# Token scalars transposed into another PSUM bank, the prologue's loads and low parts in another order, some of VectorE's low parts asked for one slab sooner

## What is computed

```python
for l in range(DEPTH):
    h = _rms_norm(x, norm_mix_pre[l])
    y = _hybrid_mixer(h, positions, w_in[l], conv_w[l], a_log[l], dt_bias[l], gdn_norm[l], w_out[l], topk)
    x = x + _rms_norm(y, norm_mix_post[l])
    h = _rms_norm(x, norm_x_pre[l])
    mem_n = _rms_norm(mem, norm_mem[l])
    y = _memory_cross_attention(h, mem_n, w_xq[l], w_xkv[l], w_xo[l])
    x = x + _rms_norm(y, norm_x_post[l])
    h = _rms_norm(x, norm_ffn_pre[l])
    y = _swiglu(h, w_gu[l], w_down[l])
    x = x + _rms_norm(y, norm_ffn_post[l])
```

```python
q = _rope(a_q.reshape(B, S, ATT_HEADS, ATT_HEAD_DIM), positions)
k = _rope(a_k.reshape(B, S, ATT_KV_HEADS, ATT_HEAD_DIM), positions)
qi = _rope(i_q.reshape(B, S, IDX_HEADS, IDX_DIM), positions)
ki = _rope(i_k.reshape(B, S, 1, IDX_DIM), positions)[:, :, 0]
y_a = _dsa_attention(q, k, v, qi, ki, i_w * (IDX_HEADS ** -0.5), topk)
qkv = _causal_conv_silu(b_qkv, conv_w)          # four taps, then silu
o_b = _gated_delta_rule(bq, bk, bv, g, beta)
y = jax.nn.sigmoid(g_a) * y_a + jax.nn.sigmoid(g_b) * y_b
return y @ w_out
```

## Time and profile before

| | |
|---|---|
| runs | 1144.62, 1144.62, 1147.76 us |
| the profiled execution | 1147.81 us, its span 1146.0 us |
| PE busy | 1121.3 us, 98% of the span |
| POOL, ACT, DVE busy | 678.3, 567.2, 559.1 us |
| mean granted clock of TensorE | 0.993 of full speed |
| chain that ended last | PE 92%; DMA 2%; DVE 2%; ACT 1%; POOL 1% |

### The profile page before, as it was taken

How to read it: one execution, slowest core, us unless ns; L and a number is a source line. 1 busy time by engine, 2 the same in 40 slices (tenths; PEclk the granted TensorE clock), 3 DMA queues, 4 the chain that set the end, 5 groups by cost and what they waited for, 6 DMA issues and landing times.

```text
span 1146.0 us, 19832 instructions
## 1 busy us (share of the span) xinstructions
PE 1121.3 (98%) x8108; PEld 1043.6 (91%) x8112; DVE 559.1 (49%) x1042; ACT 567.2 (49%) x894; POOL 678.3 (59%) x355
## 2 busy tenths in 40 slices
PE   8899999999999899999998999999999999999997
PEld 6899999998798799999998999999988978999997
DVE  5678566445412543534545856683634235211333
ACT  7445764434554534444463467543445545444443
POOL 4776567617684347754586658575187634576433
PEclk9899999999999999999998999999999999999999
DMA  7344334524543545555553444455155344555553
GB/s 280 130 165 148 131 133 161 176 65 151 203 149 127 178 170 184 184 185 185 185 177 134 148 143 153 123 176 161 40 199 185 129 149 160 188 184 184 184 183 112
DMA packets 63338, 183.41 MB, mean 160 GB/s; under 512 B 18576, under 2 KB 19088, under 8 KB 63248
## 3 DMA queue, kind: packets, MB, share of 16 engines
q1 hardware_dynamic: 47936, 172.51, 42.9%
q10 hardware_dynamic: 15312, 9.64, 3.1%
HBM read 179.51 MB, written 2.62 MB: 159 GB/s over the span
## 4 chain that ended last, share of the span: by engine, by line
PE 92%; DMA 2%; DVE 2%; ACT 1%; POOL 1%; issue 1%; SPq 0%; DVEq 0%; POOLq 0%; ACTq 0%
PE psum L476 26%; PE psum L477 26%; PE psum L478 26%; DMA sb_raw<-weights 2%; PE psum L613 1%; PE psum L904 1%; PE psum L883 1%; PE psum L657 1%; PE psum L640 1%; PE psum L550 1%; PE psum L789 1%; PE psum L796 1%; PE psum L624 1%; PE psum L750 1%; PE psum L741 1%
## 5 line engine op out<-in xcount | busy, mean ns | idle before, releaser
L379 POOL TENSOR_TENSOR sb_low<-sb_raw,sb_high 128x1024 fp32r<-128x1024 f32 x261 | 627.7, 2416 | 355.3 <-ACT sb_high L369 347.0
L369 ACT ACTIVATE sb_high<-sb_raw 128x1024 fp32r<-128x1024 f32 x322 | 340.4, 1061 | 468.0 <-DMA sb_raw<-weights 406.6
L476 PE MATMUL psum<-sb_h_high,sb_high 128*128 128x256 f32 x1664 | 472.0, 284 | 1.3 <-DVE sb_low L379 1.3
L478 PE MATMUL psum<-sb_h_high,sb_low 128*128 128x256 f32 x1664 | 469.7, 282 | 0.0
L477 PE MATMUL psum<-sb_h_low,sb_high 128*128 128x256 f32 x1664 | 469.3, 282 | 0.0
L476 PEld LDWEIGHTS psum<-sb_h_high,sb_high 128*128 128x128 f32 x1664 | 314.4, 189 | 3.7 <-issue 2.2
L477 PEld LDWEIGHTS psum<-sb_h_low,sb_high 128*128 128x128 f32 x1664 | 313.3, 188 | 0.9
L478 PEld LDWEIGHTS psum<-sb_h_high,sb_low 128*128 128x128 f32 x1664 | 312.6, 188 | 0.0
L379 DVE TENSOR_TENSOR sb_low<-sb_raw,sb_high 128x1024 fp32r<-128x1024 f32 x61 | 94.2, 1557 | 30.0 <-ACT sb_high L369 29.5
L1926 DVE SCALAR_TENSOR_TENSOR sb_sq<-sb_th,psum 128x512 f32<-128x512 f32 x22 | 15.1, 688 | 140.3 <-ACT sb_th L1360 140.3
L1697 DVE SCALAR_TENSOR_TENSOR sb_conv<-psum,sb_param,sb_conv 128x255 f32<-128x255 f32 (+1 forms) x144 | 58.3, 474 | 48.6 <-ACT sb_conv L1172 48.5
(11 more groups left out here) (278 smaller groups left out, 1594.0 us busy)
## 6 DMA issues: line engine op xcount, KB each, us to landing
sb_raw<-weights SPq DMA_DIRECT2D x322, 512.0 KB, 3.2
sb_pre_gain<-pre_gains ACTq DMA_DIRECT2D x6, 512.0 KB, 5.1
sb_post_gain<-post_gains ACTq DMA_DIRECT2D x6, 512.0 KB, 3.7
sb_kx<-mem SPq DMA_DIRECT2D x2, 512.0 KB, 4.3
sb_x<-x SPq DMA_DIRECT2D x1, 1024.0 KB, 11.2
t_dram<-sb_sq ACTq DMA_DIRECT2D x4, 256.0 KB, 2.9
out<-sb_x SPq DMA_DIRECT2D x4, 256.0 KB, 2.1
m_dram<-sb_m ACTq DMA_DIRECT2D x8, 64.0 KB, 2.0
```

The lines of the kernel that those rows point to most:

```text
L369: nc.scalar.activation(high[:, n % HIGHS, :], raw[:, n % RAWS, :], ACT.Copy).then_inc(high_ready, 1)
L379: eng.tensor_tensor(low[:, k, :], raw[:, k, :], high[:, n % HIGHS, :].bitcast(F32), ALU.subtract).then_inc(low_ready[k], 1)
L476: pe.matmul(out, a[0], b[0], start=start, stop=False, **kw)
L478: return pe.matmul(out, a[1], b[0], start=False, stop=stop, **kw)
```

## The change

It has four pieces.

1. The token scalars are transposed into bank 3 in place of bank 6. Bank 3 holds the angles while the rotary tables are made, in layer 0; no claim of the layer has used it by then.
2. SP loads slabs 0, 1, 2, then x, then the positions, then slabs 3 and 4. Low part 3 is now DVE's. ACT makes high part 3 after the squares of x. In DVE's `prenorm` a call `low_parts(4)` is added behind the loop over the two tiles, under the condition that the loop's variable `c` is 0; the loop leaves it at 1, so the call is not made.
3. In the norm behind `out`, DVE asks for low parts up to two slabs ahead of `out` in place of one, ahead of the wait for the sum of squares.
4. Ahead of the first `silu` of the feed-forward part DVE asks for low parts up to three slabs ahead in place of two.

```diff
-            return n in (0, 2, HALVES + 4) or (part, i, b) in (("xv", 2, 0), ("xv", 2, 1), ("xv", 3, 0), ("xo", 3, 1))
+            return n in (0, 2, 3, HALVES + 4) or (part, i, b) in (("xv", 2, 0), ("xv", 2, 1), ("xv", 3, 0), ("xo", 3, 1))
...
             for n in range(RAWS):
+                sp.dma_start(raw[:, n, :], weights[n]).then_inc(raw_loaded[n], 16)
                 if n == 2:
+                    sp.dma_start(x, x_in.rearrange("(c p) d -> p c d", p=P)).then_inc(x_loaded, 16)
                     sp.dma_start(y_t[:, 0:S].bitcast(I32), pos_in.broadcast_to([P, S])).then_inc(pos_loaded, 16)
-                    sp.dma_start(x, x_in.rearrange("(c p) d -> p c d", p=P)).then_inc(x_loaded, 16)
-                sp.dma_start(raw[:, n, :], weights[n]).then_inc(raw_loaded[n], 16)
...
                 wide(("k", 0), h, (dve_rope, "k"))
-                o = claim("small_tok", (dve_gate, "x"), (6,))
+                o = claim("small_tok", (dve_gate, "x"), (3,))
                 pe.wait_ge(*act_copy.at(layer, "small"))
...
-            highs(act, done, HIGHS)
+            highs(act, done, HIGHS - 1)
...
                         square_x("mix", c, half)
                 if layer == 0:
+                    highs(act, done, HIGHS)
                     for j in range(4):
...
+                    if (layer, which, c) == (0, "mix", 0):
+                        low_parts(4)
                     if between is not None:
                         between()
...
-                        low_parts(ahead(product, 2 if part == "x" else 1))
+                        low_parts(ahead(product, 2))
...
                 for i in range(FF_SLOTS):
-                    low_parts(ahead(("gate", i), 2))
+                    low_parts(ahead(("gate", i), 2 if i else 3))
```

## The result

The changed kernel takes 1153.85 us (median of 7 runs, 1150.26 to 1155.72), where the kernel before takes 1145.76 us on the same chip (7 runs, 1143.39 to 1148.2). The ratio is 1.0067, with a 95% interval of 1.0054 to 1.0081: slower by 7.7 us by the ratio, by 8.1 between the medians. The forecast was 1153.7 us.

The account below looks back on a forecast made before the run. PE, busy 1121.3 of 1146.0 us, bounds the kernel, so only its standstills and half clock matter. 1147.8 - 12.2 + 8.2 + 5.1 + 5.8 + 1.9 - 2.95 = 1153.7 us; range of 8 in 10: 1147.8 to 1157.5.

Parts of the forecast that it names:

- waits and half clock at L568: Token-scalar transposes, both layers: PE's two 3.03 us waits and the 3.1 and 3.05 us of clock go, -12.2 us.
- `bv 0` standing still: First matmul of bv 0 waits for DVE's taps of bq 3, 4.13 and 4.06 us by layer, +8.2 us.
- half clock at `bv 0`: PE's clock falls in each of the two bv 0 stops, costing 2.55 us each, +5.1 us.
- slab 3 late, less the wait at slab 4: Prologue: slab 3 starts 7.4 us later, at 28.2 us; 1.57 us come back at slab 4, +5.8 us.
- half clock in the prologue: PE stands from 20.2 to 28.2 us before slab 3, so its clock falls, +1.9 us.
- waits at slabs 75 and 99: Earlier requests for low parts 75 and 99 remove PE's waits of 0.28, 1.35 and 1.32 us, -2.95 us.
- rotation behind `bk 2`, layer 1: Layer 1's bk 2: no wait was forecast here, 0 us in the sum.
- The base: Whole kernel: sum made from the profiled 1147.8 us; the 3.2 us down to the median not carried over.
- The two readings of the earlier trace: Half clock timed from PE's restart (6.2 us, loss 3.1) or from the clock's fall (6.8 us, loss 2.55).
- rival B: Stops at bv 0 come without half clock, the prologue's with little: 1148.5 us, chance 0.14.
- the arrival of x: Prologue: x, loaded behind slab 2, was taken to land at 15.2 us, between 14.4 and 15.45.
- Most claims keep their reader: Bank claims behind the token scalars: the shifted round gives bv 0 a late new reader, no other new reader late.

Follow-up runs that it names:

- x1: Kernel before with only the token scalars moved to bank 3, which shifts the round of later bank claims: 1147.3 us, ratio 1.0015.
- x2: Kernel before with the token scalars in bank 3 and the round of later claims set back as before: 1137.07 us, ratio 0.9927.
- x10: The full change plus one line setting the round of claims behind the token scalars back as before: 1141.67 us, ratio 0.9966.
- x11: Kernel before with bank 3 (round shifted) and the two earlier asks for low parts, old prologue: 1146.72 us, ratio 1.0012.
- x3: Kernel before with the prologue piece alone (load order, low part 3 on DVE, high part 3 later): 1150.57 us, ratio 1.0048.
- x7: The full change plus 16 matmuls nobody reads ahead of bv 0 in each layer: 1150.08 us, ratio 1.0042.
- x8: Kernel before with bank 3, round kept, earlier asks, new load order and high part 3, POOL's low part 3 behind the norm's roots: 1132.62 us, ratio 0.9895.
- x5: The full change with POOL's low parts behind the norm of x held until DVE's low part 3 in layer 0: 1150.63 us, ratio 1.0049.
- x6: The full change with the added low-part call really made, between the norm of x and the angles: 1146.69 us, ratio 1.0015.
- x4: Kernel before with only the two earlier asks, for low parts 75 and 99: 1142.54 us, ratio 0.9974.

## Why the forecast was right, step by step

Each term of the sum stands here beside what the profile after shows.

| term | forecast | measured |
|---|---|---|
| waits and half clock at L568 | -12.2 | gone; -5.9 in layer 0, -3.0 and -2.7 in layer 1 |
| `bv 0` standing still | +8.2 | +8.1 (4.06 and 4.00) |
| half clock at `bv 0` | +5.1 | +5.1 (3.0 and 2.1) |
| slab 3 late, less the wait at slab 4 | +5.8 | prologue together +5.7 |
| half clock in the prologue | +1.9 | 1.5, within those 5.7 |
| waits at slabs 75 and 99 | -2.95 | gone; 0.4 left elsewhere |
| rotation behind `bk 2`, layer 1 | 0 | +1.45 |

**The base.** The sum was made on the profiled execution of before, 1147.8 us, and its 3.2 us over the median were not carried over, as clock that the other runs did not lose. The profiled execution after is 1153.87 us, 6.1 above that of before, and the median 1153.85. The choice held: the median of after lies at its profiled time.

**The transposes.** Right, in place and in size: no bracket at L568 in either layer, and full clock behind it. In layer 1 the logits gained 2.7 us on the transposes, where 3.05 were foreseen for the clock.

**The banks.** Right, and the step that decided the sign. The forecast read the start of `bv 0` against the end of the taps in a trace in which nobody waited for them; 4.13 and 4.06 us by that, 4.06 and 4.00 in the result. The experiments show it to be the shifted round: x1 and x2 differ in nothing else, and neither do the full change and x10.

**The clock.** The two readings of the earlier trace rows gave 2.55 or 3.1 us for each stop. The middle of the layers is 2.55 as taken, though by luck: it is 3.0 in one and 2.1 in the other, because the clock fell 3.2 and 1.4 us after PE's last matmul and not 2.4 in both. Other kernels with stops of this kind had stretches of 3.4 us (x11, a loss of 1.6 and 1.7), and two with the prologue's stop had 10.2 (x3, x10). What the term is as a mean over many executions is not settled; rival B, in which it is missing altogether, did not come.

**The prologue.** The mechanism was right, the size was not: slab 3 began at 26.97 us, not 28.2, and slab 4 at +5.7, not +7.7. The term that was mis-sized is the arrival of x. It was taken at 15.2 us for the 512 KB put ahead of it; DVE saw it at 14.14. The chain of waits shows why: x's transfer stands in it as

```profile
3.14 10.87 DMA sb_x<-x
```

and it was issued at 3.16 before. Slab 2 has taken the place of the positions on SP, so x was not issued any later, and its 10.9 us did not grow with slab 2 ahead. The rest follows from that: low part 2 began at 14.26 us where 15.3 was taken, low part 3 was asked for at 23.93 where 25.1 was, and ended at 26.92 where 28.2 was. The stretching by POOL was sized right, 1.77 us over the 1.22 alone for 1.9 (28.2 less 26.3): POOL's second low part had just begun when DVE's came. The half clock cost 1.5 us for 1.9 (it fell at 23.1 us, not 22.6), and slab 4 comes 1.67 us behind the start of the transposes, where 1.91 was counted.

**The low parts.** Slabs 75 and 99 wait no more. The asks alone gave the 3.0 us of the forecast; in the company of the other pieces part of that was already gone (x11).

**What was missed.** "Most claims keep their reader" is true of `bk 2` in layer 1, but the reader was late. DVE's timeline of after and POOL's beside it, then the same of before, ahead of the rotation of `q 1`:

```profile
637.75 2.41 DVE L1685 TENSOR_TENSOR sb_sel_bias<-sb_sel_bias,sb_const 128x128 bf16<-128x128 bf16 x1
...
632.81 7.21 POOL L379 TENSOR_TENSOR sb_low<-sb_raw,sb_high 128x1024 fp32r<-128x1024 f32 x3 [2.21 <-ACT sb_high L369]
```

```profile
637.53 0.29 DVE L1682 TENSOR_TENSOR sb_sel_bias<-sb_sel_bias,sb_const 128x128 bf16<-128x128 bf16 x1
...
637.65 2.43 POOL L379 TENSOR_TENSOR sb_low<-sb_raw,sb_high 128x1024 fp32r<-128x1024 f32 x1 [0.25 <-ACT sb_high L369]
```

An instruction of 0.29 us took 2.41, up to the end of POOL's third low part in a row (637.63 to 640.02 us), which had begun 0.12 us before it. Before the change DVE's came first, by 0.12 us, and took 0.29. DVE's chain ran late from there: the rotation of `q 3` began at 659.56 where it had begun at 656.66, and PE waited 1.45 us for it. The step of the forecast that failed is that it let the slack of unchanged readers stand.

The other traces bear this out, in layer 1 of each. In the profile after and in x7 this instruction starts 0.12 and 0.18 us behind the start of a low part of POOL's and takes 2.41 and 2.39 us. In the eleven other kernels, before among them, it starts before POOL's next low part or together with it (in x8), and takes 0.29 us. The wait for `sb_gates` is in the lists of those two and of none of the eleven, whatever the round of the banks. So a shift of a few tenths of a microsecond between POOL and DVE decides it. No experiment moved this one instruction alone.

Two misses, -2.0 us in the prologue and +1.45 at `bk 2`, all but cancel. That the forecast lies within 0.2 us of the median is luck; its steps are good to 1 or 2 us each.

**Still open.** The three pieces alone sum to +4.2 us, together they give +7.7. About 2.6 us of the difference show in bank 3 and the asks without the prologue (x11: +1.4 where -1.3 would be the sum), and up to 1.45 us is `bk 2`. Whether x11's surplus is late low parts of h or clock is not shown; intervals of 1.2 us either way do not tell. Why the clock falls sooner or later behind the same stop is open too.

## What to carry to other kernels

Where buffers are handed out in turn, a fixed choice at one place moves every later one, up to the next fixed place; before moving one, write down who reads each buffer last, and how long before its next user asks. A wait can be costed before it exists: subtract the start of the waiting instruction from the end of the one it will wait for, in a trace in which neither waits, and then reckon separately what the clock does behind a stop of that length. An operation handed to another engine stands behind everything that this engine has to do ahead of it in its program, so the place of the request matters more than the engine: the same low part cost 6.6 or 1.9 us of waiting by its place in DVE's program, and 0.2 by a good place in POOL's.

## What the runs showed of the hardware

- **The same stop does not always cost the same clock.** Stops of PE of 3.0 to 4.1 us came with 6.8 us at 1.2 GHz (before, after, x1, x5, x6), with 3.4 (x4, x11, x3 in layer 1) or with none (x3 in layer 0). In the first group the clock fell 1.1 to 3.3 us after PE's last matmul, and 2.1 to 3.1 us were lost behind the restart. In the second it fell 3.6 to 4.5 us after it, about at the restart or behind it, and 1.6 to 1.7 us were lost. A window of x4 behind its stop of 3.0 us in layer 0, and the next one:

```profile
48.20:51.40 3.20, 3.20 (x17) 3.20 (x17) 1.30 (x7) 3.07 (x6) 1.09 (x1) 0.50 0.00 0
51.80:54.00 2.20, 2.20 (x22) 2.20 (x20) 2.13 (x4) 1.06 (x1) 0.36 (x1) 1.00 0.22 54
```

- **Short VectorE instructions stretch the most beside GpSimd.** A subtraction of 128 x 1024 went from 1.22 to 2.99 us, one operation on 128 x 128 bf16 from 0.29 to 2.41, and the first of four operations of 128 x 512 from 0.75 to 2.50 (x8). What is added is 1.8 to 2.1 us in each, so in proportion the shortest instruction suffers most. Each of the three had started 0.1 to 0.5 us behind a low part of 2.4 us on GpSimd. The other side pays as well: POOL's third low part in the prologue, beside which DVE's ran, took 3.36 us.
- **A load put ahead did not delay the load behind it.** x, issued at 3.14 us, landed 10.87 us later and was seen at 14.14 us, where it had been seen at 14.46 us. Ahead of it were 512 KB more of weights and 128 KB less, the positions, which had moved behind it; the two were not tried apart.
